# Layer 1's dilated attention: V as the weights of its products with the softmax maps, the two heads' outputs in the two halves of PSUM's partitions

## The chip, the cores and the metric

The kernel runs on one core of one Trainium2 chip. The metric is the device time of one launch in microseconds; a time is the median of several runs. Five engines work from their own in-order queues and meet through semaphores: TensorE (PE; its weight loads are shown apart, as PEld), VectorE (DVE), ScalarE (ACT), GpSimd (POOL) and SyncE (SP), which issues the DMAs.

## What is computed

Two decoder layers over 1024 tokens of 1024 channels, float32 in and out, with an error that rules out plain low-precision products. Layer 1 projects the normalised input into three convolution streams and into q, k and v of 8 heads of 64 channels. The change touches the attention of layer 1:

```python
def dilated_attention(q, k, v, slopes):
    # three branches (window, dilation) = (128,1), (512,4), (2048,16)
    for window, dil in D_BRANCHES:
        o, lse = dilated_branch(q, k, v, slopes, window, dil)   # softmax over the branch's keys, times v
        outs.append(o); lses.append(lse)
    wts = jax.nn.softmax(jnp.stack(lses, axis=0), axis=0)       # branches weighted by their denominators
    return jnp.sum(wts[..., None] * jnp.stack(outs), axis=0)

x = x + jnp.concatenate([yc, yd], axis=-1) @ od_w_out           # yc: convolution, yd: attention
```

The kernel computes the three branches as one softmax: a key that k branches see gets log k added to its score, keys that none sees get a large negative number.

## The kernel before

Large products are done as three products of float32r halves (high x high, high x low, low x high), with weights of 128x128 and 512 moved columns. The two feed-forward parts and the projections take most of the time. The work is written out by hand for every engine in one block (`trunk`), and the order of the queues is the order of the code.

Layer 1's attention goes over `UNITS` = 4 units of two heads (m = 0 and 1) and in each over `NT` = 8 tiles of 128 queries; n = 8u + i counts the 32 tiles. Tile i has i + 1 key blocks of 128, as the attention is causal. For one tile and head:

- `score` (TensorE): the stacked queries times two stacks of keys, float32r, into PSUM banks 0 and 1 (m = 0) or 2 and 3 (m = 1). It runs two tiles ahead.
- `biased` (VectorE): adds the bias table, writes the negated scores to `PR` and their minimum to `NMX`.
- `expo` (ScalarE): the exponential, with the sum in `DEN`. The result is not divided yet.
- `turn` (TensorE): i + 1 transposes of 128x128 into banks 4 to 6, which go round in threes.
- `turned` (ScalarE for the first four blocks, VectorE for the others): copies the turned map to `PTL` in SBUF.
- `weigh` (TensorE): the turned map block as the weight, 64 columns of V moved, plain float32, summed over the blocks into 64 columns of bank 7. The result has queries on the partitions.
- `denominator` and `scaled` (VectorE): 1/DEN as one number per partition, and the product into `Y`.

TensorE's order in tile n is turn(0,n), score(0,n+2), weigh(0,n-1), turn(1,n), score(1,n+2), weigh(1,n-1). VectorE's is denominator(0,n-1), biased(0,n+1), denominator(1,n-1), scaled(1,n-2), biased(1,n+1), copies of turned(0,n), scaled(0,n-1), copies of turned(1,n). Both heads share bank 7, so `weigh` of one head waits for `scaled` of the other. In tile 6 of a unit VectorE also computes the next unit's two bias tables (`next_bias`).

Behind the attention comes the output projection. Its convolution half (`u_tile`, 16 tiles of 12 products, added to X by VectorE) needs nothing of the attention. Between its tiles 1, 3, 5 and 7 `turn_y` turns `Y` back, channels on the partitions, in 8 transposes for each of 4 blocks of 128 channels; ScalarE (`y_hi`) and VectorE (`y_lo`) split them into halves in HH and HL, which `out_part` uses. SyncE loads the next output weights once the last product with V is done.

Layer 0's attention uses the same `weigh` with 128 moved columns.

Of the kernel before, what the change touches and what calls it, by code (L numbers as in the profile page):

```python
# [82 lines left out]
def trunk(nc, a, out):  # L83
    ctx = ExitStack()
    with ctx:
# [23 lines left out]
        Y = at("Y", [P, NT, HALF], F32, oA)  # L109
        WOh = at("WOh", [P, 2, D], F32R, oV)  # L110
# [175 lines left out]
        YJ = at("YJ", [P, P], F32, oK + 4 * KB)  # L286

# [75 lines left out]
        o_pe = [sems("o_peA"), sems("o_peB")]  # L363
        o_ok = [sems("o_okA"), sems("o_okB")]
# [90 lines left out]
        def weighed(L, m, n):  # L455

            return bank(7 if n < FILL_FROM and n % 2 else 6)[:, 0:P] if L == 0 else bank(7)[:, 0:HD]
# [128 lines left out]
        def _(sp):  # L586
# [13 lines left out]
            for L in range(2):  # L600
# [195 lines left out]
                if L == 0:  # L796

                    sp.wait_ge(od_pe[0], 24)
                else:

                    for m in range(2):
                        sp.wait_ge(o_pe[m][1], TILES0)
# [277 lines left out]
        def _(pe):  # L1080
# [85 lines left out]
            def weigh(L, m, n):  # L1166

                u, i = n // NT, n % NT
                if n == 0:
                    pe.wait_ge(bank_free[L], 3 * NT)  # L1170
                pe.wait_ge(t_ea[m][L], n + 1)
                if L == 1 and i >= 4:
                    pe.wait_ge(t_ed[m][1], 4 * u + i - 3)
                if L == 0:
                    pe.wait_ge(o_ok[0][0], n + (1 if n < FILL_FROM else 2))
                else:
                    pe.wait_ge(o_ok[1 - m][1], n + 2 + m)
                w, off = (P, u * P) if L == 0 else (HD, u * P + HD * m)
                turned = PTL[m][i % 2] if L else PT[i % 2]
                for j in range(i + 1):  # L1180
                    last = pe.matmul(weighed(L, m, n), turned[:, P * j:P * j + P], V[:, j, off:off + w],  # L1181
                                     start=(j == 0), stop=(j == i))
                last.then_inc(o_pe[m][L], 1)


            for L in range(2):
                for f in (ja_free if L == 0 else []) + [s_mx[0][L], s_mx[1][L]]:
                    pe.sem_inc(f, 1)
                for f in (t_pe[0][L], t_pe[1][L], o_ok[0][L], o_ok[1][L]):
# [4 lines left out]
            for L in range(2):  # L1194
# [135 lines left out]
                def out_block(n):  # L1330

                    q, t = n // NT, n % NT
                    if n == 0:
                        pe.wait_ge(uh_lo, 4)

                        pe.wait_ge(o_ok[0][0], 1 + FILL_FROM)
# [7 lines left out]
                    elif n == BLOCKS_IN + 2:  # L1344
                        pe.wait_ge(o_ok[0][0], 2 + TILES0)
# [7 lines left out]
                def turn_y(j):  # L1353
                    if L == 0:
                        pe.wait_ge(y_ok, j + 1)
                        if j < 2:

                            for m in range(2):
                                pe.wait_ge(s_mx[m][0], 1 + TILES0)
                    else:  # L1360
                        pe.wait_ge(o_ok[0][1], 2 + 8 * UNITS)
                        pe.wait_ge(o_ok[1][1], 2 + 8 * UNITS)
                    if j >= 2:
                        pe.wait_ge(yt_lo, 4 * L + j - 1)
# [4 lines left out]
                if L == 0:  # L1369
                    for u in range(UNITS):  # L1370
                        b, g = u % 2, NT * u
                        following = stacks_before(0, u + 1)
                        for i in range(NT):
# [9 lines left out]
                            if g + i > 0:  # L1383
                                weigh(0, 0, g + i - 1)
# [8 lines left out]
                    weigh(0, 0, TILES0 - 1)  # L1393
                else:
                    for u in range(UNITS):
                        b, g = u % 2, NT * u
                        following = stacks_before(1, u + 1)
                        for i in range(NT):
# [3 lines left out]
                            turn(1, 0, u, i)  # L1402
                            if i == NT - 2 and more:
# [5 lines left out]
                            if g + i > 0:  # L1409
                                weigh(1, 0, g + i - 1)  # L1410
# [5 lines left out]
                            if g + i > 0:  # L1416
                                weigh(1, 1, g + i - 1)
                    for m in range(2):
                        weigh(1, m, TILES0 - 1)
# [6 lines left out]
                else:  # L1426
                    pe.wait_ge(uh_lo, 8)
                    pe.wait_ge(wo_lo, WO_AT[1] + 1)
                    for t in range(NT):
                        if t == 1:  # L1430
                            for m in range(2):
                                pe.wait_ge(o_ok[m][1], 2 + TILES0)
# [151 lines left out]
        def _(act):  # L1584
# [124 lines left out]
            for L in range(2):  # L1709
# [135 lines left out]
                def split_o(g):  # L1845
# [3 lines left out]
                    elif g == 1:  # L1849
                        for m in range(2):  # L1850
# [1016 lines left out]
```

## Time and profile before

| | us |
|---|---|
| median of 3 runs | 2194.12 (2192.97 to 2194.75) |
| span of the profiled execution | 2193.9 |
| TensorE busy in it | 2156.8 (98%) |
| TensorE's weight loads busy | 1809.3 (82%) |
| VectorE busy | 1323.6 (60%) |
| ScalarE busy | 900.8 (41%) |
| GpSimd busy | 860.1 (39%) |
| chain that ended last: TensorE / issue | 81% / 13% |

The span is that of one execution, from its first to its last instruction. Matmuls are pipelined and their ends are modelled, so two records that follow each other overlap in the tables, and the busy time of TensorE says less than the distances between starts. A plain float32 product shows as two records, a float32r product and a transpose as one.

### The profile page before, as it was taken

The numbers are of one execution on the slowest core, as the hardware profiler recorded it, in microseconds if no ns is written. First come the engines' busy times: TensorE is split into PE (matmuls) and PEld (weight loads), VectorE is DVE, ScalarE is ACT, GpSimd is POOL, SyncE is SP. The second block draws the span as 40 slices with busy tenths as digits, with TensorE's granted clock in tenths as the row PEclk, the third lists the DMA queues.
The fourth block names the chain that finished last, engine by engine and source line by source line (L and its number), as shares of the span: only waits on it lengthen the run. The fifth ranks groups of instructions, "written<-read, shape, count | busy, mean of one in ns | idle before, by whom it ended". The sixth has DMA issues, their size and how long they took to land.

```text
span 2193.9 us, 30208 instructions
## 1 busy us (share of the span) xinstructions
PE 2156.8 (98%) x10572; PEld 1809.3 (82%) x10572; DVE 1323.6 (60%) x1829; ACT 900.8 (41%) x1497; POOL 860.1 (39%) x563
## 2 busy tenths in 40 slices
PE   8999999999999999999999999999999999999999
PEld 7877798888888887888888888988888888887887
DVE  4345875765555555558597356656765555555555
ACT  4134874443333334435332148642433333334433
POOL 1022442466666672002244133220466777652000
PEclk9999999999999999999999999999999999999999
DMA  5011421055555448674312111311155555557665
GB/s 190 7 59 41 125 78 30 20 183 201 193 190 167 155 152 285 193 244 155 115 39 58 49 58 40 116 39 39 54 195 184 187 179 170 172 172 273 194 195 192
DMA packets 229536, 295.56 MB, mean 135 GB/s; under 512 B 11825, under 2 KB 133169, under 8 KB 229169
## 3 DMA queue, kind: packets, MB, share of 16 engines
q1 hardware_dynamic: 229136, 294.04, 41.0%
q8 instruction: 68, 1.11, 0.2%
q14 instruction: 44, 0.35, 0.1%
q10 hardware_dynamic: 288, 0.05, 0.0%
HBM read 208.06 MB, written 77.59 MB: 130 GB/s over the span
## 4 chain that ended last, share of the span: by engine, by line
PE 81%; issue 13%; DVE 2%; ACT 2%; POOL 2%; DMA 1%; SPq 0%; POOLq 0%; DVEq 0%; ACTq 0%
PE PS L1533 12%; PE PS L1532 12%; PE PS L1531 12%; PE PS L1558 6%; PE PS L1559 6%; PE PS L1560 6%; PE PS L1181 4%; PE PS L1083 4%; PE PS L1085 4%; PE PS L1084 4%; PE PS L1162 2%; POOL QRS L989 1%; PE PS L1137 1%; PE PS L1138 1%; PE PS L1248 1%
## 5 line engine op out<-in xcount | busy, mean ns | idle before, releaser
L2136 DVE TENSOR_TENSOR LINEl<-LINE,HIGH 128x1024 fp32r<-128x1024 f32 x154 | 195.1, 1274 | 167.5 <-ACT HIGH L1589 167.1
L1589 ACT ACTIVATE HIGH<-LINE 128x1024 fp32r<-128x1024 f32 x154 | 163.0, 1060 | 235.8 <-PE PS L1560 209.9
L1558 PE MATMUL PS<-HIGH 128*128 128x512 f32 x616 | 240.3, 390 | 4.4 <-ACT KEEP L1589 4.0
L1560 PE MATMUL PS<-HIGH,LINEl 128*128 128x512 f32 x616 | 239.7, 389 | 0.0
L1559 PE MATMUL PS<-LINEl,HIGH 128*128 128x512 f32 x616 | 239.6, 389 | 0.0
L2136 DVE TENSOR_TENSOR SLOTl<-BLOCKS,RING 128x512 fp32r<-128x512 f32 x168 | 156.0, 929 | 95.3 <-ACT RING L1589 90.7
L921 POOL TENSOR_TENSOR ST<-ST 128x512 f32<-128x512 f32 x132 | 192.5, 1459 | 32.4 <-DMA ST<-in_ffn_w_down 23.8
L1589 ACT ACTIVATE RING<-BLOCKS 128x512 fp32r<-128x512 f32 x168 | 105.9, 630 | 227.2 <-PE PS L1533 223.1
L2136 DVE TENSOR_TENSOR SLOTl<-SLOT,RING 128x512 fp32r<-128x512 f32 x126 | 132.7, 1053 | 88.1 <-ACT RING L1589 87.9
L1558 PEld LDWEIGHTS PS<-HIGH 128*128 128x128 f32 x616 | 115.6, 188 | 29.5 <-DVE LINEl L2136 2.9
L989 POOL TENSOR_TENSOR QRS<-QMS,EXPO 128x8 f32<-128x8 f32 x32 | 52.1, 1638 | 220.8 <-DVE QMS L2397 220.2
L1560 PEld LDWEIGHTS PS<-HIGH,LINEl 128*128 128x128 f32 x616 | 115.6, 188 | 23.9
L1559 PEld LDWEIGHTS PS<-LINEl,HIGH 128*128 128x128 f32 x616 | 115.7, 188 | 23.8
L1589 ACT ACTIVATE RING<-SLOT 128x512 fp32r<-128x512 f32 x126 | 79.2, 630 | 125.5 <-PE PS L1533 115.2
L1531 PE MATMUL PS<-B1h,RING 128*128 128x512 f32 x336 | 130.7, 389 | 0.0
L1532 PE MATMUL PS<-B1l,RING 128*128 128x512 f32 x336 | 130.7, 389 | 0.0
L1533 PE MATMUL PS<-B1h,SLOTl 128*128 128x512 f32 x336 | 130.7, 389 | 0.0
L893 POOL TENSOR_TENSOR SLOT<-BLOCKS 128x512 f32<-128x512 f32 x42 | 55.3, 1316 | 189.8 <-DMA BLOCKS<-in_ffn_w_up 189.8
L926 POOL TENSOR_TENSOR RST<-MSQ,EXPO 128x1 f32<-128x1 f32 x32 | 22.8, 714 | 233.9 <-DVE MSQ L2154 233.9
L1083 PE MATMUL PS<-WQh,HH 128*128 128x512 f32 x256 | 102.5, 400 | 0.6 <-DVE U L2449 0.6
L1085 PE MATMUL PS<-WQh,HL 128*128 128x512 f32 x256 | 99.9, 390 | 0.0
L1084 PE MATMUL PS<-WQl,HH 128*128 128x512 f32 x256 | 99.7, 389 | 0.0
(418 smaller groups left out, 5807.1 us busy)
## 6 DMA issues: line engine op xcount, KB each, us to landing
LINE<-hidden SPq DMA_DIRECT2D x154, 256.0 KB, 2.7
hidden<-HID SPq DMA_DIRECT2D x44, 512.0 KB, 4.4
ST<-in_ffn_w_down SPq DMA_DIRECT2D x44, 512.0 KB, 4.1
sums<-ST SPq DMA_DIRECT2D x22, 1024.0 KB, 6.2
hidden<-ST SPq DMA_DIRECT2D x22, 1024.0 KB, 6.7
LINE<-sums SPq DMA_DIRECT2D x88, 256.0 KB, 2.9
BLOCKS<-in_ffn_w_gate SPq DMA_DIRECT2D x42, 512.0 KB, 4.0
BLOCKS<-in_ffn_w_up SPq DMA_DIRECT2D x42, 512.0 KB, 5.3
```

Of the source, the lines that this page charges most:

```text
L921: nc.gpsimd.tensor_tensor(dst, x, y, op).then_inc(st_sum, 1)
L1083: pe.matmul(dst, lh, rh, start=first, stop=False)
L1084: pe.matmul(dst, lh, rl, start=False, stop=False)
L1085: return pe.matmul(dst, ll, rh, start=False, stop=last)
L1531: pe.matmul(dst, lh, rh[:, k, :], start=k == 0 and not adds_on, stop=False, skip_group_check=adds_on)
L1532: pe.matmul(dst, lh, rl[:, k, :], start=False, stop=False, skip_group_check=adds_on)
L1533: last = pe.matmul(dst, ll, rh[:, k, :], start=False, stop=k == 3, skip_group_check=adds_on)
L1558: pe.matmul(dst, hi[:, 0, ts], hi[:, 1, :], start=j == 0 and not adds_on, stop=False, skip_group_check=adds_on)
L1559: pe.matmul(dst, hi[:, 0, ts], lo[:, 1, :], start=False, stop=False, skip_group_check=adds_on)
L1560: pe.matmul(dst, lo[:, 0, ts], hi[:, 1, :], start=False, stop=j == NJ - 1, skip_group_check=adds_on).then_inc(dn_pe, 1)
L1589: return nc.scalar.activation(dst, src, ACT.Copy, **kw)
L2136: return v.tensor_tensor(dst, src, hi.bitcast(F32), ALU.subtract)
```

## The change

- V becomes the weight of the products (`weigh_unit`): for block j and head m the weights are V's 64 columns of that head and the turned map block is moved, 128 columns. The result has channels on the partitions: head 0 in partitions 0 to 63 of bank 7, head 1 in 64 to 127. The two heads alternate, block by block, and one semaphore counts both.
- These products stand at the end of a tile, behind the turns of both heads' maps, instead of one after each score.
- A division per query is now one along the columns. VectorE writes the reciprocals of both heads' sums, each 64 times side by side, into `RB` (128x128, `denominators_by`); TensorE turns it into bank 7 (`turn_by`, after turn(0,n)); VectorE copies it to `RS` and multiplies the products by it into `YT` (`unit_scaled_out`).
- `YT` has channels on the partitions already: layer 1's `turn_y` goes, and `y_hi` and `y_lo` read `YT` in SBUF.
- VectorE's queue: both `biased` stand together at the head of a tile behind `denominators_by`, and `unit_scaled_out` at its end.
- Layer 0's part does the same work as before under simpler names.

```diff
-            def weigh(L, m, n):
+            def turn_by(n):
+                if n == 0:
+                    pe.wait_ge(bank_free[1], 3 * NT)
+                pe.wait_ge(o_ok[1], n + 2)
+                pe.wait_ge(rb_ok, n + 1)
+                pe.transpose(unit_by(), RB[n % 2][:], IDN[:])
+
+            def weigh_unit(n):
+                u, i = n // NT, n % NT
+                for m in range(2):
+                    pe.wait_ge(t_ea[m][1], n + 1)
+                    if i >= 4:
+                        pe.wait_ge(t_ed[m][1], 4 * u + i - 3)
+                for j in range(i + 1):
+                    for m in range(2):
+                        off = u * P + HD * m
+                        last = pe.matmul(unit_out()[HD * m:HD * m + HD, :], V[:, j, off:off + HD],
+                                         PTL[m][i % 2][:, P * j:P * j + P], start=(j == 0), stop=(j == i))
+                last.then_inc(o_pe[1], 1)
...
                             turn(1, 0, u, i)
+                            if g + i > 0:
+                                turn_by(g + i - 1)
                             if more:
                                 score(1, 0, b, g, i + 2)
-                            if g + i > 0:
-                                weigh(1, 0, g + i - 1)
                             turn(1, 1, u, i)
                             if more:
                                 score(1, 1, b, g, i + 2)
                             if g + i > 0:
-                                weigh(1, 1, g + i - 1)
-                    for m in range(2):
-                        weigh(1, m, TILES0 - 1)
+                                weigh_unit(g + i - 1)
+                    turn_by(TILES0 - 1)
+                    weigh_unit(TILES0 - 1)
...
                         u_tile(0, t)
-                        if t in (1, 3, 5, 7):
-                            turn_y(t // 2)
...
+                    else:
+                        act.wait_ge(o_ok[1], 2 + NT * (j + 1))
+                        copy(HH[:, 4 + j, :], YT[:, j, :]).then_inc(yt_hi, 1)
...
-                    def denominator(m, n):
-                        c = m + 2 * (n % 2)
-                        dve.wait_ge(s_ex[m][1], n + 1)
-                        att.did(v.reciprocal(RDN[:, c:c + 1], DEN[:, c:c + 1]))
+                    def denominators_by(n):
+                        c = 2 * (n % 2)
+                        for m in range(2):
+                            dve.wait_ge(s_ex[m][1], n + 1)
+                        by = DEN[:, c:c + 2].rearrange("p (m o) -> p m o", o=1).broadcast_to([P, 2, HD])
+                        v.reciprocal(RB[n % 2][:].rearrange("p (m d) -> p m d", d=HD), by).then_inc(rb_ok, 1)
...
-                        att.wait()
-                        dve.wait_ge(o_pe[m][1], n + 1)
-                        v.tensor_scalar(Y[:, i, off:off + HD], weighed(1, m, n), RDN[:, c:c + 1], None, ALU.mult).then_inc(o_ok[m][1], 1)
+                    def unit_scaled_out(n):
+                        u, i = n // NT, n % NT
+                        dve.wait_ge(o_pe[1], n + 1)
+                        att.link(v.tensor_copy(RS[n % 2][:], unit_by()))
+                        v.tensor_tensor(YT[:, u, P * i:P * i + P], unit_out(), RS[n % 2][:], ALU.mult).then_inc(o_ok[1], 1)
...
                         if n > 0:
-                            denominator(0, n - 1)
+                            denominators_by(n - 1)
                         if i == NT - 1:
                             att.wait()
                         if more:
                             biased(0, b, g, i + 1)
-                        if n > 0:
-                            denominator(1, n - 1)
-                        if n > 1:
-                            scaled(1, n - 2)
-                        if more:
                             biased(1, b, g, i + 1)
                         turned(0, n)
                         if i == NT - 2 and u + 1 < UNITS:
                             next_bias(0)
-                        if n > 0:
-                            scaled(0, n - 1)
                         turned(1, n)
                         if i == NT - 2 and u + 1 < UNITS:
                             next_bias(1)
+                        if n > 0:
+                            unit_scaled_out(n - 1)
```

## Rows read from the trace of the kernel before

**Rows 1.** windows of layer 1's attention: PE, PEld, DVE, ACT, POOL busy, clock, DMA

```profile
1318.00:1340.00 22.00, 21.18 (x161) 19.56 (x162) 15.38 (x54) 20.73 (x48) 8.85 (x6) 1.00 0.21 50
...
1440.00:1456.00 16.00, 14.92 (x119) 14.56 (x118) 5.91 (x17) 6.11 (x9) 4.55 (x1) 0.90 0.01 2
```

**Rows 2.** waits in 1318 to 1456 us: total us, times, longest

```profile
DVE Y L2573 <- PE PS L1181: 43.8, 53, 3.3
...
PE PS L1181 <- DVE Y L2573: 3.3, 5, 0.8
```

**Rows 3.** groups of the stage, TensorE: busy us, mean ns, idle before

```profile
L1162 PE MATMUL PS<-IDN,PR 128*128 128x128 f32 x288 | 42.4, 274 | 0.7 <-ACT PR L1798 0.7
L1181 PE MATMUL PS<-V,PTB 128*128 128x64 f32 x320 | 41.7, 279 | 3.8 <-DVE Y L2573 3.3
...
L1181 PE MATMUL PS<-V,PT 128*128 128x64 f32 x256 | 32.7, 271 | 0.0
```

**Rows 4.** timeline (start us, length us, engine, line), weight loads of one tile

```profile
1378.85 1.64 PEld L1181 LDWEIGHTS PS<-V,PT 128*128 128x128 f32 x14
...
1380.35 0.91 PEld L1162 LDWEIGHTS PS<-IDN,PR 128*128 128x128 f32 x8
...
1381.23 0.19 PEld L1137 LDWEIGHTS PS<-K,QX 128*128 128x128 f32 x1
```

**Rows 5.** timeline, first weight load of a seven-block score tile and the next products

```profile
1329.13 0.19 PEld L1137 LDWEIGHTS PS<-K1X,QX 128*128 128x128 f32 x1
...
1329.88 1.04 PEld L1181 LDWEIGHTS PS<-V,PTB 128*128 128x128 f32 x8
```

**Rows 6.** timeline of TensorE in layer 0, 128 moved columns

```profile
315.10 2.02 PE L1181 MATMUL PS<-V,PT 128*128 128x128 f32 x16
316.88 0.42 PE L1137 MATMUL PS<-K,QST 128*128 128x384 f32 x1
```

**Rows 7.** timeline, the last tile: products, VectorE's scaling, next products

```profile
1449.64 1.86 PEld L1181 LDWEIGHTS PS<-V,PTB 128*128 128x128 f32 x16 [0.65 <-issue]
...
1451.75 0.28 DVE L2573 TENSOR_SCALAR Y<-PS,RDN 128x64 f32<-128x64 f32 x1 [2.23 <-PE PS L1181]
...
1452.15 2.95 PEld L1181 LDWEIGHTS PS<-V,PTB 128*128 128x128 f32 x16 [0.65 <-issue]
```

**Rows 8.** groups of the stage, VectorE

```profile
L2566 DVE RECIPROCAL RDN<-DEN 128x1 f32<-128x1 f32 x64 | 10.0, 157 | 0.0
...
L2424 DVE SCALAR_TENSOR_TENSOR BIAS<-DIST,SM,MASK 128x1024 f32<-128x1024 f32 x6 | 8.6, 1437 | 0.0
...
L2440 DVE CUSTOM_DVE_ANT_0 PR<-PS,BIAS 128x1024 f32<-128x1024 f32 x6 | 7.3, 1212 | 0.0
...
L2561 DVE COPY PT<-PS 128x128 f32<-128x128 f32 x8 | 2.3, 288 | 0.6 <-PE PS L1162 0.6
...
L2440 DVE CUSTOM_DVE_ANT_0 PR<-PS,BIAS 128x128 f32<-128x128 f32 x6 | 1.7, 286 | 0.1
```

**Rows 9.** timeline, two VectorE operations of which the second needs the first

```profile
1303.20 0.69 DVE L2396 TENSOR_REDUCE QSS<-SQ 128x8 f32<-128x512 f32 x1 [10.49 <-ACT SQ L1830]
...
1303.92 0.17 DVE L2397 TENSOR_SCALAR QMS<-QSS 128x8 f32<-128x8 f32 x1
```

**Rows 10.** timeline, weight loads around one turn of Y

```profile
1462.30 0.19 PEld L1085 LDWEIGHTS PS<-WOh,UL 128*128 128x128 f32 x1
...
1462.53 1.02 PEld L1366 LDWEIGHTS PS<-IDN,Y 128*128 128x128 f32 x8
...
1463.52 0.19 PEld L1083 LDWEIGHTS PS<-WOh,UH 128*128 128x128 f32 x1
...
1463.86 0.19 PEld L1085 LDWEIGHTS PS<-WOh,UL 128*128 128x128 f32 x1
```

**Rows 11.** windows at the stage's end, columns as in the first group

```profile
1450.00:1454.00 4.00, 3.46 (x26) 3.35 (x26) 0.35 (x2) 0.00 (x0) 0.00 (x0) 0.85 0.02 4
1454.00:1458.00 4.00, 4.00 (x14) 3.42 (x14) 0.28 (x1) 0.00 (x0) 0.00 (x0) 0.50 0.32 87
```

More of the change, by code:

```diff
@@ L286, in trunk @@
         YJ = at("YJ", [P, P], F32, oK + 4 * KB)
+        RB = [at(f"RB{b}", [P, P], F32, oK + 4 * KB + 512 * b) for b in range(2)]
+        RS = [at(f"RS{b}", [P, P], F32, oK + 5 * KB + 512 * b) for b in range(2)]
         SM = small("SM", 16 + 64)
@@ L453, in turn_bank, with weighed, unit_out, unit_by @@
             return bank(4 + c) if L == 0 else bank(4 + TURNS.index((m, i, c)) % 3)
-        def weighed(L, m, n):
-            return bank(7 if n < FILL_FROM and n % 2 else 6)[:, 0:P] if L == 0 else bank(7)[:, 0:HD]
+        def weighed(n):
+            return bank(7 if n < FILL_FROM and n % 2 else 6)[:, 0:P]
+        def unit_out():
+            return bank(7)[:, 0:P]
+        def unit_by():
+            return bank(7)[:, P:2 * P]
         def block_out(n):
@@ L1164, in turn, with weigh @@
                 last.then_inc(t_pe[m][L], 1)
-            def weigh(L, m, n):
+            def weigh(n):
                 u, i = n // NT, n % NT
                 if n == 0:
[L1170 to L1179, printed above, removed]
+                    pe.wait_ge(bank_free[0], 3 * NT)
+                pe.wait_ge(t_ea[0][0], n + 1)
+                pe.wait_ge(o_ok[0], n + (1 if n < FILL_FROM else 2))
                 for j in range(i + 1):
-                    last = pe.matmul(weighed(L, m, n), turned[:, P * j:P * j + P], V[:, j, off:off + w],
+                    last = pe.matmul(weighed(n), PT[i % 2][:, P * j:P * j + P], V[:, j, u * P:u * P + P],
                                      start=(j == 0), stop=(j == i))
-                last.then_inc(o_pe[m][L], 1)
+                last.then_inc(o_pe[0], 1)
+            def turn_by(n):
[16 more added lines that the diff above has]
+                last.then_inc(o_pe[1], 1)
             for L in range(2):
@@ L1188, in _ @@
                     pe.sem_inc(f, 1)
-                for f in (t_pe[0][L], t_pe[1][L], o_ok[0][L], o_ok[1][L]):
+                for f in (t_pe[0][L], t_pe[1][L], o_ok[L]):
                     pe.sem_inc(f, 2)
@@ L1353, in turn_y @@
                 def turn_y(j):
[L1354 to L1359, printed above, removed]
-                    else:
[L1361 to L1364, printed above, removed]
+                    pe.wait_ge(y_ok, j + 1)
+                    if j < 2:
+                        for m in range(2):
+                            pe.wait_ge(s_mx[m][0], 1 + TILES0)
+                    else:
+                        pe.wait_ge(yt_lo, j - 1)
                     for t in range(NT):
@@ L1430, in _ @@
                         if t == 1:
-                            for m in range(2):
-                                pe.wait_ge(o_ok[m][1], 2 + TILES0)
+                            pe.wait_ge(o_ok[1], 2 + TILES0)
                         u_tile(0, t)
-                        if t in (1, 3, 5, 7):
-                            turn_y(t // 2)
                     pe.wait_ge(wo_lo, WO_AT[1] + 2)
@@ L1849, in split_o @@
                     elif g == 1:
-                        for m in range(2):
-                            act.wait_ge(o_pe[m][1], 8 * UNITS)
+                        act.wait_ge(o_pe[1], TILES0)
                     else:
@@ L1884, in scaled @@
                     c = 2 * (i % 4)
[L1885 to L1887 removed]
+                    act.wait_ge(o_pe[0], n + 1)
+                    act.wait_ge(o_ok[0], n + 2)
+                    nc.scalar.activation(YJ[:], weighed(n), ACT.Square, scale=RDN[:, c:c + 1],
                                          accum_out=YSS[:, n:n + 1]).then_inc(y_sq, 1)
[L1889 removed]
+                    copy(Y[:, i, P * u:P * u + P], weighed(n), scale=RDN[:, c:c + 1]).then_inc(o_ok[0], 1)
                 def y_hi(j):
[L1892 to L1894 removed]
+                    if L == 0:
+                        act.wait_ge(yt_pe, j + 1)
+                        copy(HH[:, j, :], PS[:, 1024 * (j % 2):1024 * (j % 2) + 1024], scale=SUBG[:, 0:1]).then_inc(yt_hi, 1)
+                    else:
+                        act.wait_ge(o_ok[1], 2 + NT * (j + 1))
+                        copy(HH[:, 4 + j, :], YT[:, j, :]).then_inc(yt_hi, 1)
                 def score_done():
@@ L2603, in _ @@
                             next_bias(1)
-                    denominator(0, TILES0 - 1)
-                    scaled(1, TILES0 - 2)
-                    scaled(0, TILES0 - 1)
-                    denominator(1, TILES0 - 1)
-                    scaled(1, TILES0 - 1)
+                        if n > 0:
+                            unit_scaled_out(n - 1)
+                    denominators_by(TILES0 - 1)
+                    unit_scaled_out(TILES0 - 1)
                 def split_o(g):
```

43 lines of the change are left out of this document (18 added, 25 removed).

## The prediction

> **What bounds the kernel now.** I read the page's busy times first: TensorE is busy 98% of the span and the chain that ended last is 81% TensorE, so time is won or lost where TensorE's queue gets shorter or starts to wait. Then the stage by windows: layer 1's attention runs from about 1318.3 to 1455.0 us, 136.7 us for 32 unit tiles of two heads, at the full granted clock but for its last microseconds [rows 1]. TensorE looks full there, ScalarE nearly so at the start, VectorE at two thirds. A busy TensorE is not a TensorE at its peak (a record lasts longer than the distance to the next), so I priced its work by distances between weight loads. Last I read the waits: the longest is VectorE's for the weighed values, 43.8 us in 53 times, and it costs nothing, because the reverse one, TensorE for VectorE's scaling, is only 3.3 us in 5 times [rows 2]. That pair of rows is what the change touches.
>
> TensorE's work in the stage: 288 turns of map blocks and 576 records of products with V (a plain fp32 product is two records) [rows 3]. Eight turns take 1380.35 to 1381.23, 0.11 each; fourteen product records 1378.85 to 1380.35, 0.107 each [rows 4]. A score tile of 7 key blocks takes 1329.13 to 1329.88, 0.107 a block [rows 5]; with some 0.04 a tile for the start, 62 tiles and 280 blocks make about 33. Sum: 31.7 + 61.6 + 33 + 0.5 for the last q/k turns = 127. So 9 to 10 us of the 136.7 are waits and start-up; about 3 of those (start, low clock at the end) stay, and 6 can go.
>
> **The products themselves.** Before, the turned map is the weight (128 columns) and V moves 64 columns; after, V is the weight (64 columns) and the map moves 128. The record count stays 576. Layer 0 moves 128 columns in the same form: sixteen records from 315.10 to 316.88, 0.111 each [rows 6]. So a record that moves 128 columns costs what it did: one after another, 576 x 0.111 = 63.9, +2.3. What can gain is the halves: m = 0 writes partitions 0 to 63, m = 1 64 to 127, and the code alternates them. No row has a product of 64 weight columns, so the bounds are both ends: two heads' records one after another (63.9) or side by side (32.0, a gain of 29.6). I take side by side: records already lie over one another (0.11 apart), the halves share no column of the array and no partition of the output, the weights are half as wide, and every second record belongs to the other half. It is the least secure choice of this prediction.
>
> The Trainium skill says the same in "TensorEngine Tiling (Array Packing)", Key Properties: different tiles can load and multiply in parallel. No run here shows it yet. "TensorE: Matmul & The Clock Gate", Measured speedup vs the span model, gives 2.38 times for three column tiles, 0.79 of ideal; by that the products would take 40 instead of 32, and my sum would come out 8 us higher.
>
> **The hand-off, which is the main term.** Follow the two queues. TensorE after, tile n: turn(0,n), turn_by(n-1), score(0,n+2), turn(1,n), score(1,n+2), weigh_unit(n-1). VectorE: denominators_by(n-1), biased(0,n+1), biased(1,n+1), copies of turned maps, unit_scaled_out(n-1). Now unit_scaled_out(n-1) waits for the last TensorE work of tile n, and behind it in VectorE's queue stand the next reciprocals and biased(0,n+2). TensorE's next turn_by waits for the first two, and score(0,n+3) waits for biased(0,n+2). Before, biased(0) stood ahead of every scaling of the newest tile and each head's product was followed by other TensorE work, so nobody waited. After, each tile closes a ring:
> - products to VectorE: the last of sixteen loads starts at 1451.31, its slot ends at 1451.42 and VectorE starts at 1451.75, 0.33 later; 0.06 more since 128 columns leave later: 0.39 [rows 7];
> - copy of the turned reciprocals, 0.288 as the 128x128 copy [rows 8], and 0.03 until a dependent operation starts (1303.89 to 1303.92) [rows 9];
> - the multiplication, 0.29 (a full tensor-tensor like the 128x128 bias form), next operation 0.08 before its end: 0.21;
> - denominators_by: 128 elements of reciprocal. Rows have only 128x1, 0.157; bounds are that and a 128x128 copy, 0.288. I take the upper, less the 0.08 overlap: 0.21;
> - biased(0): 0.286 for one key block to 1.212 for eight, even steps between [rows 8];
> - to TensorE: VectorE's end at 1452.03 to the load at 1452.15, 0.12 [rows 7].
> Ring = 1.25 + B. TensorE fills it with turn(0,n) alone (0.11 a block; turn_by, the new one, fits inside). Exposed per tile: 1.25 + B - T. Over a unit's 8 tiles B sums to 8 x 0.749 = 6.0 and T to 36 x 0.11 = 4.0, so 10 + 6.0 - 4.0 = 12.0 a unit, 48 for four. The first two tiles have no ring (-3.1), the last two no biased (-1.5), the tail one more hand-off (+1.3): **+44.8 us**, 1.4 a tile. This holds whichever way the products run.
>
> **Smaller terms.**
> - In tile 6 of a unit VectorE also builds two bias tables of 1.437 [rows 8], about 1.2 each in sequence here, and copies 384 columns twice, all ahead of unit_scaled_out. Worked through, VectorE comes 1.1 late after side-by-side products, not late after serial ones: 3 x 1.1 + 0.5 = +3.8, or +0.5.
> - Before the 31 groups of products TensorE goes from full width to halves. Bounds: 0 (the loads run ahead as now) and 0.4 (the queue empties: record end and one hop). I take one hop, 0.12: +3.7. On the way back the ring hides it. The skill's tiling page (same section) says that a change of tiling mode drains TensorE; that speaks against this change, and 0.4 each would be 12, 8 above my sum.
> - Y's 32 turns in the output projection go. Loads come 0.23 apart; from the turn's first load 1462.53 to the second after it 1463.86 are 1.33 where 0.45 would be [rows 10]: 0.88 each, four: -3.5. ScalarE and VectorE split the same values from SBUF, before they are needed; no DMA is added or moved.
> - Old waits of products for VectorE and of products for a fresh copy go: -6, from above.
> - ScalarE: per tile two copies, two exponentials of up to 1.14, a stack copy: at most 3.8 us where the new tile takes 5 to 6. It is near the bound at the start of a unit now [rows 1], and is not after.
>
> **Sum**, made against the profiled span of 2193.9, 0.2 under the median of 2194.12: -29.6 + 44.8 + 3.8 + 3.7 - 3.5 - 6.0 = +13.2. I predict **2207.3 us**.
>
> **Rivals.**
> - *Serial halves* (the change doesn't do what it says): the two heads' records follow one another. +2.3 + 44.8 + 0.5 + 3.7 - 3.5 - 6.0 = +41.8, 2235.9. For it: every fp32 record here has its own 0.107 to 0.111 slot, whatever its shape [rows 4, 6]. Against it: no record here left half of the array free.
> - *The ring is covered, faster*: all of it hangs on the mean exposed hand-off. The other terms with side-by-side products give -31.6, so below 1.0 us a tile (instead of 1.4) the change wins. It would be so if VectorE's short operations overlap more and the reciprocal costs as its one-column form, and if products of half width reach VectorE sooner; at 0.8 a tile it is -6, 2188. Against it: B alone is 0.75 in the mean and its row is direct.
> - *Low clock*: granted clock fell to 0.85 and 0.50 at 1450 to 1458, after TensorE had done only turns and 64-column products with short waits [rows 11]. After, it waits about 1.4 of every 4.5 us. At the lower level (1.2 GHz) for half of the stage, some 98 us of work take 49 more: 2256.
>
> **How the numbers follow.** Forecast 0.48, own range 2198 to 2220: overlap of 0.8 of ideal, the entry bound and a few microseconds of low clock lie above, cheaper VectorE operations below. Serial 0.32, 2226 to 2246. Covered ring 0.10, 2180 to 2192. Low clock 0.10, above 2244. The range leaves out about the last two: 2193 to 2243. A measurement of this kernel can tell 0.2%, 4.4 us, from no change. Faster by more than that: 0.10. Within: 0.10, the low end of the forecast and the high end of the covered ring. Slower: 0.80.
>
> **What would show it.** TensorE's waits for VectorE (turn_by for YT or RB, score for NMX) should be 40 us or more in the stage, once per tile; VectorE's own wait for the products should end just before biased(0) starts. A pair of heads of 8 blocks (32 records) should take 1.8 us side by side or 3.6 in series. The stage should last about 154 us (183 in series), the output projection 3.5 less. I am wrong if biased(0) starts while the products of the tile before still run, if the stage's TensorE idle stays under 30 us, or if the granted clock is below 1.00 over whole tiles.

## The result and the profile after

The changed kernel takes **2225.5 us** (median of 4 runs, 2221.8 to 2230.0), the kernel before 2193.6 on the same chip: 1.0145 times as long, 95% interval 1.0131 to 1.0160. That is 32 us slower where 13.2 were forecast. The sign came as said, and so did the mechanism in the main; the size did not. In the profiled execution the span is 2223.7, 29.8 more than before.

The stage, from the first turn of a map to the first load of the output projection, went from 136.4 us (1318.55 to 1454.98) to 172.1 (1317.62 to 1489.75); forecast were 154. Its window in the trace of after, columns as in [rows 1]:

```profile
1318.00:1490.00 172.00, 128.70 (x1080) 100.23 (x1080) 106.82 (x253) 101.86 (x213) 43.33 (x23) 0.96 0.16 50
```

TensorE is busy for 129 of 172 us, where before it was busy for nearly the whole stage [rows 1], and its mean granted clock is 0.96. The waits of this window (us in total, times, longest), which answer to [rows 2]:

```profile
DVE RS L2594 <- PE PS L1207: 56.4, 29, 3.5
...
PEld PS L1195 <- DVE YT L2595: 39.7, 30, 2.0
PE PS L1195 <- DVE RB L2589: 34.2, 31, 1.8
...
PE PS L1148 <- DVE NMX L2461: 8.2, 19, 0.8
```

VectorE still waits for the products. New is the reverse: TensorE stands 34.2 us in 31 times before the turn of the reciprocals (L1195) and 8.2 more, in 19 times, before the scores: a wait for VectorE in every tile. Each waits for the other: the ring. Here is one turn of it, after the 12 product records of a three-block tile (start, length, engine, line; in brackets the idle time before, and what ended it):

```profile
1375.02 0.63 PEld L1207 LDWEIGHTS PS<-PT,V 128*64 128x64 f32 x12
...
1375.82 0.53 PEld L1173 LDWEIGHTS PS<-IDN,PR 128*128 128x128 f32 x5 [0.17 <-issue]
...
1375.94 0.29 DVE L2594 COPY RS<-PS 128x128 f32<-128x128 f32 x1 [2.27 <-PE PS L1207]
...
1376.27 0.29 DVE L2595 TENSOR_TENSOR YT<-PS,RS 128x128 f32<-128x128 f32 x1
1376.47 0.94 DVE L2589 RECIPROCAL RB<-DEN 128x128 f32<-128x128 f32 x1
...
1377.34 0.89 DVE L2461 CUSTOM_DVE_ANT_0 PR<-PS,BIAS 128x768 f32<-128x768 f32 x1
1377.53 0.14 PEld L1195 LDWEIGHTS PS<-IDN,RB 128*128 128x128 f32 x1 [1.18 <-DVE YT L2595]
...
1378.29 0.19 PEld L1148 LDWEIGHTS PS<-K,QST 128*128 128x128 f32 x1 [0.62 <-DVE NMX L2461]
```

TensorE has its own turns of maps to do from 1375.82 (five, of which the profile shows the loads up to 1376.35), and then stands until RB is there, and again until biased(0) has given NMX. The two groups of VectorE that matter (busy, mean ns of one), against [rows 8]:

```profile
L2589 DVE RECIPROCAL RB<-DEN 128x128 f32<-128x128 f32 x32 | 30.1, 942 | 0.0
L2594 DVE COPY RS<-PS 128x128 f32<-128x128 f32 x32 | 9.3, 290 | 56.4 <-PE PS L1207 56.4
```

The copy is what the 288 ns row said. The reciprocal takes 0.942 us; I had bounded it by 0.157 and 0.288.

The last products of the stage, 32 records, and the load behind them:

```profile
1487.85 1.73 PEld L1207 LDWEIGHTS PS<-PTB,V 128*64 128x64 f32 x32
...
1489.75 0.19 PEld L1094 LDWEIGHTS PS<-WOh,UH 128*128 128x128 f32 x1 [0.17 <-issue]
```

1.90 us with the change of width, so the halves do run side by side. The products' two groups show the form, 64 columns of weights:

```profile
L1207 PE MATMUL PS<-PTB,V 128*64 128x128 f32 x320 | 23.1, 295 | 0.0
...
L1207 PE MATMUL PS<-PT,V 128*64 128x128 f32 x256 | 17.5, 279 | 0.0
```

### The profile page after: what moved, and what is told of

Read it like the earlier page. It is cut to its first block, busy times and chain, and to the rows that moved or that the text cites. A ratio compares the mean times of both kernels' runs of the same rounds, so it can differ in the third digit from the quotient of the medians.

```text
span 2223.7 us, 30153 instructions
## 1 busy us (share of the span) xinstructions
PE 2150.1 (97%) x10572; PEld 1783.9 (80%) x10572; DVE 1333.2 (60%) x1797; ACT 905.0 (41%) x1497; POOL 862.7 (39%) x563
## 4 chain that ended last, share of the span: by engine, by line
PE 78%; issue 13%; DVE 4%; ACT 2%; POOL 2%; DMA 1%; SPq 0%; DVEq 0%; POOLq 0%; ACTq 0%
PE PS L1550 12%; PE PS L1551 12%; PE PS L1552 12%; PE PS L1577 6%; PE PS L1579 6%; PE PS L1578 6%; PE PS L1094 4%; PE PS L1096 4%; PE PS L1095 4%; PE PS L1148 2%; PE PS L1207 2%; PE PS L1173 2%; PE PS L1149 1%; POOL QRS L1000 1%; PE PS L1273 1%
## 5 line engine op out<-in xcount | busy, mean ns | idle before, releaser
L2157 DVE TENSOR_TENSOR SLOTl<-SLOT,RING 128x512 fp32r<-128x512 f32 x126 | 127.3, 1010 | 87.8 <-ACT RING L1608 87.6
L1579 PEld LDWEIGHTS PS<-HIGH,LINEl 128*128 128x128 f32 x616 | 115.7, 188 | 24.1
L904 POOL TENSOR_TENSOR SLOT<-BLOCKS 128x512 f32<-128x512 f32 x42 | 55.4, 1318 | 189.7 <-DMA BLOCKS<-in_ffn_w_up 189.7
L1817 ACT ACTIVATE PR<-PR,NMX 128x256 f32<-128x256 f32 (+7 forms) x128 | 98.6, 775 | 30.0 <-DVE NMX L2461 29.9
```

The costliest lines, as they stand in the source:

```text
L1579: pe.matmul(dst, lo[:, 0, ts], hi[:, 1, :], start=False, stop=j == NJ - 1, skip_group_check=adds_on).then_inc(dn_pe, 1)
L1817: nc.scalar.activation(pr, pr, ACT.Exp, bias=NMX[:, c:c + 1], scale=-1.0, accum_out=DEN[:, c:c + 1]).then_inc(s_ex[m][L], 1)
L2157: return v.tensor_tensor(dst, src, hi.bitcast(F32), ALU.subtract)
```

## The experiments

All runs are of the whole kernel; the ratio is to the kernel before on the same chip at the same time, and "stage" is measured as above, in the profiled execution. Against the changed kernel I compare ratios, times 2194, as the medians of before lay between 2193.6 and 2196.8. The products of r6 mix the channels of the two heads, so its attention is not the reference's; it is there for its time alone. Its stage and its rows are from r6b, one more execution of the same kernel (2247.5 us).

| | ratio (95%) | over before, us | stage, us |
|---|---|---|---|
| changed kernel | 1.0145 (1.0131 to 1.0160) | +31.8 | 172.1 |
| r1 short reciprocal, copied | 1.0110 (1.0093 to 1.0127) | +24.1 | 166.1 |
| r2 heads in series | 1.0199 (1.0182 to 1.0216) | +43.7 | 188.1 |
| r3 ring open | 0.9909 (0.9892 to 0.9925) | -20.0 | 121.1 |
| r4 ring put into before | 1.0105 (1.0086 to 1.0123) | +23.0 | 160.5 |
| r5 ring open, wide reciprocal | 0.9916 (0.9887 to 0.9946) | -18.4 | 121.2 |
| r6 full width | 1.0242 (1.0215 to 1.0270) | +53.1 | 193.3 |
| r7 short reciprocal, by max | 1.0131 (1.0104 to 1.0157) | +28.7 | 169.3 |
| r8 ring open, by max | 0.9914 (0.9887 to 0.9942) | -18.9 | 121.7 |
| r9 two wide reciprocals | 1.0381 (1.0353 to 1.0408) | +83.6 | 221.3 |
| r10 reciprocal before scaling | 1.0030 (1.0019 to 1.0041) | +6.6 | 145.7 |

**Is it the ring?** Two runs: r3 opens it in the changed kernel, r4 closes it in the kernel before, whose products are untouched.

r3_ring_open (VectorE's order, and TensorE's turn_by moved):

```diff
                             turn(1, 0, u, i)
-                            if g + i > 0:
-                                turn_by(g + i - 1)
...
                             if g + i > 0:
+                                turn_by(g + i - 1)
                                 weigh_unit(g + i - 1)
...
                         if n > 0:
-                            denominators_by(n - 1)
+                            denominators_of(n - 1)        # 1/DEN, 128x2
...
                             biased(1, b, g, i + 1)
+                        if n > 1:
+                            unit_scaled_out(n - 2)
+                        if n > 0:
+                            denominators_by(n - 1)        # its copy, 64 columns a head
...
-                        if n > 0:
-                            unit_scaled_out(n - 1)
```

> The changed kernel with the ring taken apart: on VectorE both biased of a tile stand ahead of unit_scaled_out of the tile two before, with the short reciprocal of r1 (the two reciprocals ahead of biased, the broadcast copy behind unit_scaled_out); on TensorE turn_by stands directly ahead of the products, behind both turns and both scores. Theory (V as weights in halves is cheaper for TensorE and the loss is the ring alone): TensorE's work in the stage is 127 - 30 + 3.5 for the new transposes and about 0.5 a tile for the change of width both ways, some 116 with 3 of start, against 136.7; with the 3.5 of the dropped turns of Y some 15 to 25 us faster than before, 2170 to 2180. Rival (the products or the changes of width cost what the halves save): 2190 to 2200 at best. Rival (ScalarE binds once the ring is gone, its operations in the stage sum to about 98 us): not under 2170.

It takes 2176.5 us, 20 less than the kernel before. In its stage the low clock is gone, and so are TensorE's waits for RB but for one, though the products, turns and copies are all still there:

```profile
1318.00:1438.00 120.00, 112.85 (x1067) 92.91 (x1067) 93.49 (x284) 97.44 (x214) 43.92 (x23) 1.00 0.23 72
```

```profile
PE PS L1173 <- ACT PT L1607: 2.5, 5, 0.6
PE PS L1148 <- DVE NMX L2460: 2.5, 3, 0.8
PE PS L1195 <- DVE RB L2593: 0.9, 1, 0.9
```

r4_ring_in_before (edit of the kernel before):

```diff
                         if n > 0:
                             denominator(0, n - 1)
+                            denominator(1, n - 1)
+                        if n > 1:
+                            scaled(1, n - 2)
...
                             biased(0, b, g, i + 1)
-                        if n > 0:
-                            denominator(1, n - 1)
-                        if n > 1:
-                            scaled(1, n - 2)
                             biased(1, b, g, i + 1)
```

> The kernel before with only VectorE's order changed in layer 1's attention: denominator(1,n-1) and scaled(1,n-2), which waits for TensorE's last product of a tile, are put ahead of biased(0,n+1). V and the maps stay as they were. Theory (the ring alone is the loss, whichever way the products run): per tile 0.33 + 0.20 + B + 0.12 less the turn of the first map, with B 0.75 and the turn 0.5 in the mean, 0.9 x 30 less the last tiles = some 25 us slower than before, 2219. Rival (the order of the queue costs nothing by itself): 2194.

2217.9 us: two short operations moved ahead of biased(0), of which scaled(1,n-2) waits for TensorE's last product of a tile, make the kernel before 23 us slower. Its waits of the stage:

```profile
PEld PS L1137 <- DVE NMX L2440: 21.3, 22, 1.0
...
PE PS L1137 <- DVE NMX L2440: 19.0, 25, 0.9
```

Such a wait of TensorE is new in it: the kernel before has none for NMX in its stage. So order alone makes a loss of this size without the new operations, and the change as a whole (products, no turns of Y) is a gain once the order is right. No run takes the products by themselves with the ring open.

**Is it the size of the reciprocal?** r1 makes it 2 columns wide and copies it to 128.

```diff
-    v.reciprocal(RB[n % 2][:]..., by).then_inc(rb_ok, 1)
+    att.link(v.reciprocal(RDN[:, c:c + 2], DEN[:, c:c + 2]))
+    v.tensor_copy(RB[n % 2][:]..., by).then_inc(rb_ok, 1)     # by: RDN, each column 64 times
```

> The changed kernel with one edit: two reciprocals (128x2), then a broadcast copy of them into RB, instead of a reciprocal of 128x128 elements, which the trace of the changed kernel shows at 0.942 us, 32 times, between unit_scaled_out and biased(0). Theory (the ring through VectorE sets each tile, and the reciprocal stands on it): some 0.16 + 0.03 + 0.25 replace 0.86, 0.42 x 31 = 13 us less than the changed kernel, so about 18 us (0.9%) slower than before. Rival (the loss lies in TensorE, in the change between full width and halves or in its clock): the same as the changed kernel, 1.45% slower than before.

2219.8 us, 24 over before where 18 were expected. The tile RB in the trace (duration min/median/max in ns) says where the rest went:

```profile
L2590 DVE COPY RB<-RDN x32: 226/227/1627, 1319.6 to 1482.8; 128x128 f32<-128x128 f32 x32
```

and one of the long ones in the timeline:

```profile
1338.10 1.80 POOL L1007 TENSOR_TENSOR QST<-QK,QST 64x768 fp32r<-64x768 f32 x1 [4.14 <-ACT QST L1608]
1338.16 0.15 DVE L2588 RECIPROCAL RDN<-DEN 128x2 f32<-128x2 f32 x1
1338.35 1.63 DVE L2590 COPY RB<-RDN 128x128 f32<-128x128 f32 x1
1339.90 1.08 DVE L2461 CUSTOM_DVE_ANT_0 PR<-PS,BX 128x896 f32<-128x896 f32 x1
```

The copy starts while GpSimd multiplies and ends with it. The 32 copies take 15.5 us and not 32 x 0.227 = 7.3. From the reciprocal's start to the biased behind it there were 0.87 us above and should be 0.39: 31 x 0.48 = 15 less, and 8.2 back leave 7, against a measured 7.7 (6.0 in the stage). r7 replaced the copy, to see whether only copies are held up:

```diff
+    v.tensor_tensor(RB[n % 2][:]..., by, by, ALU.max).then_inc(rb_ok, 1)
```

> r1_short_reciprocal with its broadcast made by a two-operand max of the same values instead of a copy. In r1 the copy took 0.227 us mostly but up to 1.63 us when GpSimd ran at the same time, 0.486 in the mean. Theory: it is this copy that a running GpSimd holds up, and a two-operand operation (0.29 us as the other 128x128 one) is not held up: the ring loses 0.94 - 0.16 - 0.29 + 0.03 = 0.5 us a tile against the changed kernel, 31 x 0.5 = 16: 2205 to 2212. Rival: every VectorE operation on SBUF alone is held up by GpSimd, or the ring is not what sets the pace: 2217 to 2225, with some RB operations over 1 us.

2224.0 us: the rival's case. The two-operand form is held up in the same way:

```profile
1383.08 1.80 POOL L1007 TENSOR_TENSOR QX<-QK,QX 64x768 fp32r<-64x768 f32 x1 [4.19 <-ACT QX L1608]
1383.15 0.15 DVE L2588 RECIPROCAL RDN<-DEN 128x2 f32<-128x2 f32 x1
1383.34 1.69 DVE L2590 TENSOR_TENSOR RB<-RDN 128x128 f32<-128x128 f32 x1
```

The wide reciprocal of the changed kernel is not; it starts beside GpSimd and keeps its 0.94 (the 32 lie between 0.941 and 0.948):

```profile
1337.69 1.80 POOL L1007 TENSOR_TENSOR QST<-QK,QST 64x768 fp32r<-64x768 f32 x1 [4.47 <-ACT QST L1608]
1337.75 0.94 DVE L2589 RECIPROCAL RB<-DEN 128x128 f32<-128x128 f32 x1
```

These are coincidences read from the traces: no run moved GpSimd's work. By the Trainium skill ("SBUF — State Buffer", SBUF: two separate sides) VectorE and GpSimd share a pair of ports as an exclusive lock, taken by a VectorE operation in a two-port mode or with two operands in SBUF, and the loser waits for the whole instruction. The held-up copy and max agree with it (1.63 and 1.69 us, to the end of GpSimd's 1.80). Why the reciprocal was not held up is not shown here.

So neither replacement was clean. r9 and r10 leave GpSimd out of it: the same wide reciprocal, twice, and in another place.

```diff
+    att.link(v.reciprocal(RB[n % 2][:]..., by))                # r9: one more, ahead of the other
     v.reciprocal(RB[n % 2][:]..., by).then_inc(rb_ok, 1)
```

> The changed kernel with the 128-column reciprocal made twice, one behind the other, into the same place: one more operation of 0.94 us in the ring of every tile and nothing else. Theory (the ring is closed and the reciprocal's whole duration lies on it): 31 x 0.94 = 29 us more than the changed kernel, a few us more where TensorE's clock falls in the longer waits: 2252 to 2260, PE's waits for RB up by some 27 us. Rival (the reciprocal lies partly beside TensorE's own work, and the ring is longer for another reason): 15 us or less, under 2241.

```diff
-                        if n > 0:
-                            denominators_by(n - 1)             # r10: from the head of the tile
                         if i == NT - 1:
...
+                        denominators_by(n)                     # to its end
                         if n > 0:
                             unit_scaled_out(n - 1)
```

> The changed kernel with one line moved: the wide reciprocal of tile n stands ahead of unit_scaled_out(n-1), at the end of tile n, and not behind it at the head of the next tile. Same operations, same size; the reciprocal is then done while TensorE is at the products of n-1, and the ring loses 0.94 - 0.08 us. Theory: 31 x 0.86 = 27 us less than the changed kernel, up to 6 less again if the low clock goes: 2192 to 2200, about the time before. PE's waits for RB are gone and become waits for YT and NMX. If the reciprocal comes too late behind the copies of the turned maps, part of it stays on the ring: 2200 to 2212. Rival (the reciprocal is not what was under-priced): 2220 or more.

r10 lies where it was expected: 25 us less than the changed kernel for one line moved, with all operations kept. TensorE's waits for RB are gone, and these are left:

```profile
PE PS L1148 <- DVE NMX L2461: 10.6, 19, 0.9
PE PS L1195 <- DVE YT L2595: 9.5, 15, 1.7
```

r9 overshot: 52 more, not 29. TensorE's wait for RB rose from 34.2 to 60.0, or 25.8, where some 27 were expected:

```profile
PE PS L1195 <- DVE RB L2590: 60.0, 31, 2.7
```

The rest is the clock, in the main. These are the windows of the stage of r9 and of r10:

```profile
1318.00:1538.00 220.00, 151.29 (x1074) 117.39 (x1074) 137.22 (x284) 102.28 (x213) 43.11 (x23) 0.84 0.12 39
```

```profile
1318.00:1464.00 146.00, 123.03 (x1060) 94.95 (x1060) 110.24 (x261) 103.74 (x221) 44.74 (x24) 1.00 0.19 59
```

A mean of 0.84 is some 70 us at the lower of the two levels; 0.96 in the changed kernel is 14, 1.00 in r10 is none. What such a stretch costs can be read from tiles with the same work. These two windows of the changed kernel run from the copy into RS (L2594) of a unit's first tile to that of its second, in unit 0 and in unit 1:

```profile
1321.60:1326.20 4.60, 3.25 (x24) 2.43 (x25) 2.60 (x8) 3.55 (x10) 2.38 (x1) 1.00 0.02 5
1364.60:1370.80 6.20, 4.85 (x24) 3.67 (x25) 2.64 (x8) 4.51 (x10) 2.37 (x1) 0.72 0.00 0
```

From copy to copy it is 4.60 us at the full clock, and 6.16, 6.14 and 6.08 in units 1 to 3, each of which has a stretch at the lower level. In r2, where units 1 to 3 keep the full clock in this tile and unit 0 does not, it is 4.61 to 4.63 and 6.17. The fourth stretch of the changed kernel lies beside VectorE's bias tables and costs 0.2 (7.18 against 6.95). Together that is 4.8 us lost to the clock, for 14 us at the lower level.

In r9 the copies of a unit's third and fourth tile are 6.85 us apart at the full clock and 8.4 with a stretch. The 6.85 is 0.99 more than in the changed kernel (5.86), and from one reciprocal's start to the next there are 0.97 (1402.27 and 1403.24): 31 x 0.97 = 30 of the 49 us by which r9's stage is longer than the changed kernel's. I put the other 19 down to its 56 more us at the lower level, 0.34 for each; that is a remainder, near the 4.8 / 14 of the changed kernel.

The reciprocal in r10's comparison cost 26.4 - 4.8 = 22 us of the stage. From copy to copy r10 is some 0.8 us shorter in most tiles, and not at all in the three with the bias tables (7.0 against 6.95), where the reciprocal still counts.

**With the ring open, does the reciprocal still matter?**

> The changed kernel with the order of r3_ring_open (both biased ahead of the scaling of the tile before last, turn_by directly ahead of the products), but the reciprocal kept as it is, 128 columns wide, ahead of biased. It tells the order from the cheap reciprocal. Theory: the 0.94 us of the wide reciprocal counted because it lay on the ring (32 x 0.65 over my price, about 20 us). With the ring open VectorE is busy some 94 of 120 us and only gets 31 x (0.94 - 0.16 - 0.37) = 13 us more work: 2176 to 2190, PE's waits for VectorE under 20 us. Rival, that VectorE is simply too slow with it, ring or no ring: 2200 or more.

r5 (r3's order, the reciprocal wide as in the change) takes 2175.8 us, r3 2176.5, r8 2176.3, with stages of 121.2, 121.1 and 121.7: no difference. Each of r5's 32 reciprocals still lasts its time:

```profile
L2588 DVE RECIPROCAL RB<-DEN x32: 941/942/953, 1318.8 to 1435.8; 128x128 f32<-128x128 f32 x32
```

> r3_ring_open with the broadcast made by the two-operand max. The copies took 12.0 us in 32 there, 0.37 in the mean against 0.29 here, but the ring is open: theory 2172 to 2177, within a few us of r3_ring_open (2176.5). It would gain more, down to 2165, only if the held-up copies delayed TensorE there.

The operation that cost 22 us on the ring is free off it; so are the held-up copies of r3 and r8.

**Do the halves run side by side?** r2 only swaps two loops, so that head 0's records all come before head 1's.

```diff
-                for j in range(i + 1):
-                    for m in range(2):
+                for m in range(2):
+                    for j in range(i + 1):
```

> The changed kernel with the two loops of the products exchanged: all blocks of head 0, then all blocks of head 1, so that neighbouring records lie in the same half of the array. Theory (two halves run side by side only when neighbours alternate): a record goes from 0.055 us in the mean to 0.111, 576 records cost 30 us more, about 2255. Rival (a record is short because its weights are 64 columns wide, and the halves do not overlap): no change, about 2225.

r6 gives every product the full width:

```diff
-    last = pe.matmul(unit_out()[HD * m:HD * m + HD, :], V[:, j, off:off + HD], ..., start=(j == 0), stop=(j == i))
+    last = pe.matmul(unit_out(), V[:, j, u * P:u * P + P], ..., start=(j == 0 and m == 0), stop=(j == i and m == 1))
```

> The changed kernel with 128 columns of V (both heads) as the weights of every product, all summed into the same 128 partitions: the same 576 records and the same waits, but no record uses half of the array's columns, and the array never changes its width. Its products mix the two heads' channels, so that part of the attention is not what the reference computes. Theory: records follow each other at 0.111 us, so products cost about +32 us; as with r2_heads_in_series a third of that lies beside VectorE's work, and the changes of width, about 0.3 us for each of 31 groups, are saved: 2235 to 2248, weight loads of a 32-record group 3.5 us. If changes of width cost nothing: 2245 to 2255. If it was not the halves that made the records fast, it stays at 2225.

> The kernel of r6_full_width (both heads' 128 columns of V as weights, so its attention mixes channels of the two heads), once more for its trace. Theory: about 2248 us; loads of a 32-record group 3.5 us (0.111 each), no idle time from the turns to the products or back beyond what the score tiles show, 0.05 us.

The last 32 records of each and the load behind them; first r2, then r6b:

```profile
1502.32 3.09 PEld L1207 LDWEIGHTS PS<-PTB,V 128*64 128x64 f32 x32
1505.58 0.19 PEld L1094 LDWEIGHTS PS<-WOh,UH 128*128 128x128 f32 x1 [0.17 <-issue]
```

```profile
1508.15 3.65 PEld L1206 LDWEIGHTS PS<-PTB,V 128*128 128x128 f32 x32
1511.72 0.19 PEld L1094 LDWEIGHTS PS<-WOh,UH 128*128 128x128 f32 x1
```

And a group of 28, first of the changed kernel, then of r2:

```profile
1442.82 1.51 PEld L1207 LDWEIGHTS PS<-PT,V 128*64 128x64 f32 x28
```

```profile
1453.13 2.65 PEld L1207 LDWEIGHTS PS<-PT,V 128*64 128x64 f32 x28
```

From 28 to 32 records the loads grow by 0.22 us alternating and by 0.44 in series: 0.055 and 0.11 a record; at full width it is 3.57 / 32 = 0.112. It is the alternation of the halves that makes them fast. r2 is 12 us slower than the changed kernel (16 in the stage of the profiled executions), not 30, and the rows say why: 32 records with what follows take 3.26 and not 1.90 us, 1.36 more, where 32 x 0.055 are 1.76. So 0.4 a group come back, which I take (not shown) to be an overlap where the half changes. 576 x 0.055 = 32, less 31 x 0.4 = 12, less 3 beside VectorE's bias tables in tile 6 (below), are 17; the stage grew by 16. r6 grew it by 21. 33 of records, less 3 in tile 6, less the entries into halves, 31 x 0.2 = 6, are 24, and its low clock is shorter (0.99 in the mean against 0.96, some 10 us), worth 3: 21. Both sums are estimates made with the results known.

## Why the prediction was right and wrong

**Right: side by side** (the choice called least secure). A pair of heads of 8 blocks takes 1.73 us of loads where 1.8 were forecast, against 3.6 in series. r2 (3.09) and r6 (3.65) show it from the other side.

**Right: the ring**, and that it decides the sign. TensorE's waits for VectorE are 42 us, some in every tile ("40 us or more"), r4 makes the loss without the change and r3 takes it away.

**Wrong: the step that failed** is the term of denominators_by in the hand-off, mis-sized. I took 0.21 us for it, from bounds of 0.157 (one column) and 0.288 (a 128x128 copy). The ring shown above has, from step to step (the last slot ends 12 x 0.055 us after the first load at 1375.02):

| step | forecast | measured |
|---|---|---|
| last slot of the products (1375.68) to VectorE | 0.39 | 0.26 |
| copy of the turned reciprocals | 0.32 | 0.33 |
| multiplication | 0.21 | 0.20 |
| denominators_by | 0.21 | 0.87 |
| biased(0) of six blocks and the hop | 1.07 | 0.95 |
| sum | 2.20 | 2.61 |

The reciprocal is 0.66 over, the others together 0.25 under: 0.41 a tile, 31 x 0.41 = 12.7. The table is of one tile, but the 0.87 is the same throughout: from the reciprocal's start to the biased behind it all 30 tiles have 0.85 to 0.87. A row for one column and the same column count of another operation do not bound an operation that costs more per element than a copy. From 0.157 for one column and 0.942 for 128 it is 0.006 us for each further column. That "rows have only 128x1" was not right either: layer 0 of the kernel before has one of two columns (L2482, 128x2, 0.160 in the mean of 32), which would not have shown this price. Where rows have only one or two elements, the upper bound has to leave room for a cost per element of its own. r10, with the reciprocal off the ring in nearly all tiles and the rest of the change as it was, measures 145.7 for the stage, where my sum without that term gives 154 - 31 x 0.21 = 147.5. The rest of the sum held, then, to 2 us in total, but in part by luck: the other steps of the ring were 0.25 a tile too dear (31 x 0.25 = 8), the change of width too cheap (below), and r10 still has the reciprocal on the ring in three tiles.

**The clock**: "wrong if the granted clock is below 1.00 over whole tiles" came true in part. 14 us of the stage ran at the lower level, 4.8 us lost; I had it only as a rival of 62 us. In the last tile ahead of each of the four falls (1346.6, 1367.1, 1411.5, 1455.9) TensorE had stood for 1.35 to 1.55 us, as in many tiles without a fall. In r10, with shorter waits, and in r3, r5 and r8 there is none. 12.7 + 4.8 = 17.5 of the 18.8 us (32.0 - 13.2) that I was short.

**Smaller terms.**
- The entry into halves: the last score load at 1374.7 and the first product load at 1375.02 in the tile above are about 0.3 apart, where r6b, which never changes its width, has 0.12 in the same place, so 0.2 and not 0.12; the way back shows 0.17 of idle time, where r6b shows none, and is covered by the ring, as said.
- The way back is not covered in r3: my terms without any ring give a span of 2193.9 - 31.6 = 2162, r3 has 2174.6, and both changes of width at some 0.35 a tile (11 us instead of 3.7) and its 3.4 us of remaining waits for VectorE (above) make up most of the difference. The 0.4 that I kept as the bound for the entry alone is near what both ways cost.
- The trace agrees with the Trainium skill ("TensorEngine Tiling (Array Packing)", Key Properties) that the array drains at a change of mode, as r6b, without such a change, has neither gap. The 0.79 of ideal that I took from "TensorE: Matmul & The Clock Gate", Measured speedup vs the span model, is given in the Trainium skill for three column tiles of 32; with the two of 64 here the overlap is full, 0.055 a record against 0.11.
- Tile 6: VectorE comes to the products at 1395.31 without a wait, behind both bias tables, where the 24 records that began at 1392.55 (1.29 of loads) would have let it start at 1394.1. It is 1.2 late, forecast were 1.1.
- The output projection: from its first load to the first one of the feed-forward 118.9 us (1489.75 to 1608.6) after, 124.0 (1454.98 to 1579.0) before. That is 5.2 less. Before, the low clock of [rows 11] lies over the first ten or so loads, 0.43 us apart there against 0.23 after, so some 2 us of it are the clock, and about 3 are left for the turns of Y, where 3.5 were forecast.

**The rivals.** Serial halves: no; r2 is that case, and is 12 us slower still. The covered ring: r3 and r5 come out like it, 2176 where I gave 2188, but only with another order; the reciprocal at the price of "its one-column form" needs a copy beside it, and r1 is still 24 us slower than before.

## What to carry to other kernels

Before a product, a turn or a scaling is moved, follow the two queues around: if each engine's next piece of work stands behind an operation that waits for the other's last one, every short operation in between is paid in full, once per tile. The cure is order, not speed: let each engine have a tile's worth of independent work ahead of the hand-off (r3, r5: the scaling of the tile before last, behind both biased), and the same operations, even one of 0.94 us, cost nothing that these runs could tell. The change as a whole, V as the weights and no turns of Y, is worth 0.8 to 0.9% here once that is done; a division whose operand is ready early belongs ahead of the wait, not behind it (r10: one line, 25 us).

## What the runs showed of the hardware

- fp32 products with 64 weight columns into the two halves of PSUM's partitions, alternating, follow each other at 0.055 us; in series at 0.11, at full width at 0.112. Going from full width to halves costs some 0.2 us, the way back shows 0.17 of idle time; at full width throughout (r6b) there is neither.
- A reciprocal takes 0.155 to 0.160 us for 128x1 and 128x2 and 0.942 for 128x128, against 0.29 for a copy from PSUM or a multiplication of that size and 0.227 for a copy within SBUF.
- A copy or a two-operand operation of VectorE with its operands in SBUF took up to 1.6 and 1.7 us instead of 0.23 and 0.29 when it met a running GpSimd operation, and ended with it; the reciprocal did not.
- TensorE's clock fell to its lower level (1.2 GHz) for some microseconds at a time, within stages in which TensorE had stood waiting in every tile: 14 us in all in the changed kernel (42 us of waits for VectorE), 10 in r2 (40), 17 in r1 (34), 21 in r7 (35), 70 in r9 (68). In r10, with 20 us of such waits, and in r3, r5 and r8 with fewer, it stayed at the upper one (2.4 GHz). The sum of the waits does not settle it: r6b has 44 us of them and only 3 at the lower level, and r4 with 22 has only the fall at the stage's end that the kernel before has too. What a stretch cost differed: 4.60 us became 6.16 for the same tile, but 0.2 us were lost where TensorE waited for VectorE's bias tables.
